# First attention's values written in token order and gathered by group on load, and the merge's row tiles taken in the order 1, 2, 0, 3

## What is computed

```python
DILATED_GROUPS = ((128, 1), (512, 4), (2048, 16))
...
qkv = proj[..., :QKV_COLS].astype(f32).reshape(
    B, S, 3, N_GROUPS, ATTN_HEADS_PER_GROUP, HEAD_DIM)
for g, (window, dilation) in enumerate(DILATED_GROUPS):
    num, den, mx = dilated_group_attention(
        qkv[:, :, 0, g], qkv[:, :, 1, g], qkv[:, :, 2, g], table_g, window, dilation)
...
m_all = jnp.max(jnp.stack(maxes), axis=0)
wts = [jnp.exp(mx - m_all) for mx in maxes]
num_tot = sum(w[..., None] * n for w, n in zip(wts, nums))
den_tot = sum(w * d for w, d in zip(wts, dens))
o_attn = num_tot / den_tot[..., None]
```

## Time and profile before

| what | value |
|---|---|
| median of 3 runs | 2580.51 us (2579.43 to 2581.24) |
| the profiled execution | 2580.89 us |
| its span, first to last instruction | 2578.7 us |
| mean granted TensorE clock | 0.996 |
| busy: TensorE matmuls, its weight loads | 2515.9 us (98%), 2050.9 us (80%) |
| busy: VectorE, ScalarE, GpSimd | 1353.0, 1048.6, 1126.6 us |

### The profile page before, as it was taken

The page is one execution under the profiler, slowest core; times in us unless marked ns, Lnnn a source line. Parts: engine busy times, 40 slices in busy tenths (PEclk is TensorE's granted clock), DMA queues, the critical chain, the costliest instruction groups (busy, mean ns, idle before and its releaser), DMA issues.

```text
span 2578.7 us, 41776 instructions
## 1 busy us (share of the span) xinstructions
PE 2515.9 (98%) x15936; PEld 2050.9 (80%) x15936; DVE 1353.0 (52%) x2579; ACT 1048.6 (41%) x2028; POOL 1126.6 (44%) x1390
## 2 busy tenths in 40 slices
PE   7999999999999999999999999899999999999999
PEld 6997777878777777777788778788887888777787
DVE  3002254345866657576532687676666007476733
ACT  4115656555433333242113453555554114455521
POOL 3332322223433233231457545576776455454452
PEclk9999999999999999999999999999999999999999
DMA  4241111211201111011432232233334114110132
GB/s 142 83 130 46 58 58 54 67 58 49 66 21 55 35 34 51 25 58 63 164 126 82 99 103 94 92 108 104 99 107 178 43 50 143 54 34 26 34 113 84
DMA packets 226566, 198.95 MB, mean 77 GB/s; under 512 B 7104, under 2 KB 193856, under 8 KB 225856
## 3 DMA queue, kind: packets, MB, share of 16 engines
q1 hardware_dynamic: 180928, 120.60, 15.2%
q10 hardware_dynamic: 45440, 75.68, 8.1%
HBM read 150.64 MB, written 45.61 MB: 76 GB/s over the span
## 4 chain that ended last, share of the span: by engine, by line
PE 84%; DVE 8%; ACT 4%; POOL 2%; issue 1%; DMA 0%; ACTq 0%; SPq 0%; DVEq 0%; POOLq 0%
PE gemm L799 14%; PE gemm L801 14%; PE gemm L800 13%; PE gemm L1260 5%; PE gemm L1262 5%; PE gemm L1261 5%; PE scores L871 2%; PE weighted L899 1%; PE scores L1464 1%; PE weighted L1488 1%; PE probs_t L884 1%; PE scores L1338 1%; PE probs_t L1131 1%; PE probs_t L1474 1%; PE scores L1035 1%
## 5 line engine op out<-in xcount | busy, mean ns | idle before, releaser
L749 POOL CAST w_hi<-w_raw 128x512 fp32r<-128x512 f32 x266 | 189.4, 712 | 1191.5 <-PE gemm L801 1034.9
L751 POOL TENSOR_TENSOR w_lo<-w_raw,w_hi 128x256 fp32r<-128x256 f32 x532 | 441.5, 830 | 42.1
L799 PE MATMUL gemm<-h_hi,w_hi 128*128 128x512 f32 x1072 | 449.0, 419 | 3.3 <-DVE h_lo L1956 3.3
L801 PE MATMUL gemm<-h_hi,w_lo 128*128 128x512 f32 x1072 | 420.1, 392 | 0.0
L800 PE MATMUL gemm<-h_lo,w_hi 128*128 128x512 f32 x1072 | 418.9, 391 | 0.0
L1609 DVE CUSTOM_DVE_ANT_0 neg_logits<-scores,bias_tile 128x128 f32<-128x128 f32 (+1 forms) x192 | 67.6, 352 | 344.7 <-PE scores L871 339.5
L799 PEld LDWEIGHTS gemm<-h_hi,w_hi 128*128 128x128 f32 x1072 | 202.1, 189 | 50.7 <-issue 14.2
L801 PEld LDWEIGHTS gemm<-h_hi,w_lo 128*128 128x128 f32 x1072 | 201.2, 188 | 44.1
L800 PEld LDWEIGHTS gemm<-h_lo,w_hi 128*128 128x128 f32 x1072 | 202.4, 189 | 32.5 <-issue 1.7
L799 PE MATMUL gemm<-xn_hi,w_hi 128*128 128x512 f32 x288 | 117.7, 409 | 1.9 <-DVE xn_lo L2236 1.7
L2476 ACT ACTIVATE prob<-neg_logits,row_max 128x128 f32<-128x128 f32 (+1 forms) x192 | 86.8, 452 | 76.7 <-DVE row_max L1609 72.0
(11 more groups left out here) (628 smaller groups left out, 6195.5 us busy)
## 6 DMA issues: line engine op xcount, KB each, us to landing
w_raw<-in_w_in SPq DMA_DIRECT2D x73, 512.0 KB, 3.9
w_raw<-in_a_w_in SPq DMA_DIRECT2D x28, 512.0 KB, 3.8
w_raw_b<-in_a_w_in SPq DMA_DIRECT2D x20, 512.0 KB, 4.7
gates_scratch<-o_f ACTq DMA_DIRECT2D x32, 256.0 KB, 2.0
merge_gates<-gates_scratch ACTq DMA_DIRECT2D x4, 2048.0 KB, 9.7
mlp_v_scratch<-v_piece ACTq DMA_DIRECT2D x32, 256.0 KB, 2.0
mlp_v<-mlp_v_scratch ACTq DMA_DIRECT2D x16, 512.0 KB, 3.9
w_raw<-in_a_w_out SPq DMA_DIRECT2D x16, 512.0 KB, 3.2
```

Source lines behind the costliest of these rows:

```text
L749: Q(pool.tensor_copy(weight_part(u, 0, ks), raw[:, s, ks, :]))
L751: Q(pool.tensor_tensor(weight_part(u, 1, ks), raw[:, s, ks, :], weight_part(u, 0, ks).bitcast(F32), ALU.subtract), E("w_split") if ks.stop ...
L799: pe.matmul(dst, w_high, hi(k, h), start=first, stop=False)
L801: m = pe.matmul(dst, w_low, hi(k, h), start=False, stop=last)
```

## The change

Block n of the values now holds the tokens 128n to 128n + 127 in every group, and `values_scratch` is laid out by token. The grouping is done by the load: SyncE issues two DMAs of 256 KB in place of one of 512 KB, with the rows of each group's order picked from DRAM, in pieces of 512 bytes for the groups 0 and 1 and 2 KB for group 2. Each raises the semaphore by 16, so that a pair and group now counts 48. The row tiles are taken in the order 1, 2 (first slot) and 0, 3 (second slot), in TensorE's and ScalarE's programs; the waits on `stat_in` and `stat_tr` are renumbered.

```diff
-        v1_d = nc.dram_tensor("values_scratch", (PAIRS, GROUPS, P, 8, P), F32).ap()
+        v1_d = nc.dram_tensor("values_scratch", (PAIRS, GROUPS, T, P), F32).ap()
...
-        stat_slots = {14 * p + 17 + j: [(p, 2 * j), (p, 2 * j + 1)] for p in range(PAIRS) for j in range(2)}
+        stat_slots = {14 * p + 17 + i: [(p, j) for j in ((1, 2), (0, 3))[i]] for p in range(PAIRS) for i in range(2)}
...
-        def tokens(ap, g, n):
-
-            if g == 0:
-                return ap[:, n * P:n * P + P]
-            r = STRIDE[g]
-            res, part = n // (8 // r), n % (8 // r)
-            return ap.rearrange("p (l r) -> p r l", r=r)[:, res, part * P:part * P + P]
...
-                    sp.dma_start(vrows[:, gi % 2, :, :], v1_d[gi // 3, gi % 3]).then_inc(bias_in[gi % 2], 16)
+                    values = v1_d[gi // 3, gi % 3]
+                    for part in range(2):
+                        if gi % 3 == 1:
+                            dst = vrows[:, gi % 2, part:8:2, :]
+                            src = values[HALF * part:HALF * part + HALF, :].rearrange("(j r) c -> j r c", r=4)
+                        elif gi % 3 == 2:
+                            dst = vrows[:, gi % 2, 4 * part:4 * part + 4, :]
+                            src = values.rearrange("(j r) c -> j r c", r=8)[:, 4 * part:4 * part + 4, :]
+                        else:
+                            dst = vrows[:, gi % 2, 4 * part:4 * part + 4, :]
+                            src = values[HALF * part:HALF * part + HALF, :].rearrange("(n j) c -> j n c", n=4)
+                        sp.dma_start(dst, src).then_inc(bias_in[gi % 2], 16)
...
-                        high, low = tokens(h1hi[:, 2 * kp + k, :], g, n), tokens(h1lo[:, 2 * kp + k, :], g, n)
+                        high, low = h1hi[:, 2 * kp + k, n * P:n * P + P], h1lo[:, 2 * kp + k, n * P:n * P + P]
...
                 if c % 12 == 0 and p > 0:
-                    pe.wait_ge(E("stat_in"), 4 * p)
+                    pe.wait_ge(E("stat_in"), 4 * p - 2)
...
-                if j == 3 or j == 0 and p > 0:
-                    pe.wait_ge(E("stat_in"), 4 * p if j == 0 else 4 * p + 1)
+                if j == 3:
+                    pe.wait_ge(E("stat_in"), 4 * p + 3)
...
-                act.wait_ge(E("stat_tr"), 4 * p + j + 1)
+                act.wait_ge(E("stat_tr"), 4 * p + (1, 2, 0, 3).index(j) + 1)
...
-                act.dma_start(v1_d[:, g, :, n, :].rearrange("x p c -> p x c"), v_stage[n][:]).then_inc(E(f"load_{n}"), 16)
+                act.dma_start(v1_d[:, g, n * P:n * P + P, :].rearrange("x p c -> p x c"), v_stage[n][:]).then_inc(E(f"load_{n}"), 16)
```

More of the change, by code:

```diff
@@ L405, in build @@
         V_OUT = (("x_again_v_out0", 16 * KT), ("oa_in_v_out1", 16 * PAIRS), ("oa_out_v_out2", 16 * (PAIRS - 1)), ("gate_out_v_out3", 32 * 16))
-        BIAS_LOADS, UP_LOADS, C_LOADS, T_HIGHS = 32 * PAIRS * GROUPS // 2, 32, 32, 20
+        BIAS_LOADS, UP_LOADS, C_LOADS, T_HIGHS = 48 * PAIRS * GROUPS // 2, 32, 32, 20
         LOADED = (80, 80, 80, 80, 64, 64, 64, 64)
@@ L880, in transposes @@
                 gi = 3 * p + g
-                pe.wait_ge(bias_in[gi % 2], 32 * (gi // 2 + 1))
+                pe.wait_ge(bias_in[gi % 2], 48 * (gi // 2 + 1))
                 for i, hh, ti in quad:
@@ L1599, in biased @@
                 dve.wait_ge(E("s_full"), c + 1)
-                dve.wait_ge(bias_in[gi % 2], 32 * (gi // 2 + 1))
+                dve.wait_ge(bias_in[gi % 2], 48 * (gi // 2 + 1))
                 if c > 0:
```

## The result

| | median (lowest to highest) | ratio to before, 95% interval |
|---|---|---|
| before, 4 runs | 2580.88 us (2579.43 to 2582.05) | |
| changed kernel, 4 runs | 2597.89 us (2595.42 to 2598.61) | 1.0065 [1.0052, 1.0078] |

The change costs 17.0 us. The profiled execution of the changed kernel took 2595.42 us, the lowest of its four: 14.53 us over the profiled execution of before. Its span is 2593.3 us and its mean granted clock 0.992; the clocks of the other three were 0.989 to 0.991.

The account below looks back on a forecast made before the run. TensorE was taken to bound the kernel, with ScalarE's copies ending last at the row tiles. Terms -5.1 + 0 + 18.0 - 4.0 + 6.2 = +15.1 us gave 2595.6 us against the median, range 2588 to 2600.

Parts of the forecast that it names:

- Part 1: Values' matmuls on TensorE: token order shortens weight loads, saving 5.1 us, 1.6 in group 1 and 3.5 in group 2.
- the rule of the free stride: Values, group 1: a stride up to 4 float32 costs nothing, so only 3.5 us saved, 2597.2 us; chance 0.02.
- Part 2: Gather on load: 12 more DMAs on SyncE cost 0, covered by 21.4 us between issue and first need.
- Part 3: Row tiles: TensorE's tile 3 waits for ScalarE's copy of tile 0 in shared bank `MB`, four stops, +18.0 us.
- Old stops: Ahead of the next pair's first scores: TensorE's three waits for the last tile copy vanish, -4.0 us.
- I take the whole 5.5: Last pair: its 5.5 us stop is charged in full, as blend, head sums and decay scan move with TensorE.
- rival 5: Last pair's stop partly swallowed by the VectorE and ScalarE chain behind it; half of 5.5 back, 2592.8 us; chance 0.08.
- Bounds: 0 if none falls, 6.2 if all do: Clock behind the four tile 3 stops: falls to 0.50, 1.56 us lost each, +6.2 us charged.
- Rival 1: Tile 3 stops come but the clock holds behind them: +8.9, 2589.4 us; chance 0.12, with a fall behind only some.

Follow-up runs that it names:

- values_only: Changed kernel with the old order of the row tiles and its waits, keeping token-order values and the gather on load: 2576.03 us, 0.9981 of before.
- before_relaxed: Kernel before, with TensorE's wait ahead of the next pair's first scores asking for three tiles copied in place of four: 2576.99 us, 0.9986 of before.
- busy_stop: Changed kernel with 15, 17, 18 and 22 unused matmuls between tile 0 and tile 3 in the four pairs: 2588.47 us, 1.0030 of before.
- own_bank: Changed kernel with tile 3 written to the bank of the transposed probabilities, so not waiting for tile 0's copy: 2571.49 us, 0.9963 of before.
- group1_strided: Changed kernel with group 1 reading every fourth token again, its values stored by group: 2598.97 us, 1.0070 of before.
- late_loads: Changed kernel with each pair's third value load issued one place later in SyncE's order: 2597.41 us, 1.0065 of before.
- tiles_only: Kernel before with only the row tiles' order changed to 1, 2, 0, 3, values as before: 2602.34 us, 1.0083 of before.
- relaxed_wait: New values, old tile order and banks; TensorE's wait ahead of the next pair's scores asks for three tiles copied, not four: 2572.20 us, 0.9968 of before.

## Why the prediction was right

The forecast was 2595.6 us, the measured median 2597.89, inside the forecast's own range; the direction and the mechanism are as told. By its steps:

- **Part 1, -5.1 us.** Measured -5.09 us in the trace, -4.7 in values_only. Group 1's share, against the rule of the free stride, is measured alone: 1.6 us.
- **Part 2, 0.** Right. The loads land in 3.9 to 4.8 us. Issuing one takes 0.46 us (median) in place of the 0.34 assumed, which nobody waits for.
- **Part 3, stops +18.0.** 3.85, 4.25, 4.43, 5.49 forecast; 3.80, 4.21, 4.41, 5.40 measured, 17.8 in all. The working held because ScalarE's copies could be read off the trace of before at the place where tile 2 had been.
- **Old stops -4.0.** Their line is gone. Part of the same gain is to be had without the change (before_relaxed).
- **"I take the whole 5.5".** Slightly too much: 1.0 us comes back in the blend. The prediction looked at the first spread of the weights only; the fifth one waited for VectorE before, and of that wait most is gone (timeline of TensorE, before and changed):

```profile
655.83 0.47 PE L922 MATMUL max_rows<-weight_rows_last,pick 128*128 128x512 f32 x1 [1.04 <-DVE numer L1654]
```

```profile
669.61 0.47 PE L925 MATMUL max_rows<-weight_rows_last,pick 128*128 128x512 f32 x1 [0.37 <-DVE numer L1657]
```

  So rival 5 was right in kind and came to 1.0 us in place of 2.7. busy_stop against own_bank has both effects in it, 17.8 - 1.0 = 16.8, measured 17.0.
- **"Bounds: 0 if none falls, 6.2 if all do".** This is the term that was mis-sized. All four fell. They cost 6.6 us in the profiled execution and 9.4 in the medians. The price of a fall was taken from one row of before, 1.56 us behind a stop of 2.94, and then used as a ceiling. But falls are not of one length. In the profiled execution of group1_strided, pair 0's stop is the same as in the changed kernel (3.66 us against 3.65), yet the clock is low for longer:

```profile
288.00:290.00 2.00, 1.37 (x6) 0.50 0.04 12
290.00:292.00 2.00, 2.00 (x6) 0.50 0.83 217
292.00:294.00 2.00, 2.00 (x6) 0.50 1.13 345
294.00:296.00 2.00, 2.00 (x8) 0.85 0.22 81
```

In the changed kernel's profiled execution it is nearly back by the second window:

```profile
290.00:292.00 2.00, 2.00 (x10) 0.98 1.05 323
```

From tile 3 to the next scores group1_strided needs 8.8 us (timeline of TensorE, below) and the changed kernel 7.5 (294.43 - 286.95). Such a longer fall costs 1.3 us more.

```profile
288.63 1.04 PE L916 MATMUL max_rows<-consts_sb,row_den 128*66 128x128 f32 x4 [3.66 <-ACT rows_max L2493]
...
297.45 0.93 PE L874 MATMUL scores<-k_t,q_t 64*128 64x128 f32 x8
```

The same stretch can be read in every kernel that has the four stops, and set against own_bank, where the clock holds (us from the start of tile 3 to the next pair's first scores; in pair 3 to the first product behind the attention):

| profiled execution | pair 0 | pair 1 | pair 2 | pair 3 | over own_bank, sum |
|---|---|---|---|---|---|
| own_bank | 6.00 | 6.00 | 6.00 | 22.32 | |
| changed | 7.48 | 7.62 | 8.08 | 23.94 | 6.80 |
| late_loads | 7.59 | 7.62 | 8.32 | 24.05 | 7.26 |
| tiles_only | 7.64 | 8.45 | 8.27 | 24.01 | 8.05 |
| group1_strided | 8.82 | 8.54 | 8.31 | 24.04 | 9.39 |

The stops ahead of tile 3 are the same in all four to 0.02 us, and the clock behind them costs 6.8 to 9.4 us. (The 6.6 above is the changed kernel's 6.8 set against the kernel before instead.) The changed kernel's profiled execution has the cheapest falls of the four; its other three runs show a lower mean clock (0.989 to 0.991 beside 0.992) and take 1.9 to 3.2 us more. That they had just such longer falls is argued from their clocks, since only one execution of each kernel has a trace.

A part of the closeness of the total, 2.3 us, is luck: this term was too low by 3.2 us (6.2 against 9.4), and the last pair's was too high by 1.0. What would have mended it: an upper bound well over a single fall's price, such as twice, since I had one row for it and no reason for a ceiling.

The fastest versions are own_bank (2571.49) and relaxed_wait (2572.20). Both beat the kernel before by 9 us and can't be told apart; relaxed_wait is the simpler one.

## What to carry to other kernels

When work is reordered, list for each step the buffer that it writes and who empties it: two steps on one bank, one behind the other, cost the whole copy, whatever the order gains elsewhere. Check also that a wait names only the copies of the buffer about to be written; here a constant one too high cost 3.4 us, and with the new values setting it right was worth as much as the new order with a bank of its own. And a stop of TensorE can cost more than its length, here by half as much again (9.4 us on 17.0 in four stops), so it pays to have other work stand in it: 12 matmuls of the next product put there (tile3_mid_half) took 2.7 us off each stop and three of the four falls with it.

## What the hardware did that I had not expected

- The clock's fall behind a stop of the same length differs between profiled executions of two kernels: behind 3.65 and 3.66 us in pair 0 it cost 1.4 us in the changed kernel and 2.7 in group1_strided. What decides it is not shown.
- Nor does a stop's length alone tell whether the clock falls right behind it. Further on, both kernels stop for 2.29 us ahead of the same product. Here are the changed kernel's row and window (timeline of TensorE; window):

```profile
1255.96 0.70 PE L802 MATMUL gemm<-o_hi,w_hi 128*128 128x512 f32 x1 [2.29 <-DVE merge_gates L1892]
```

```profile
1256.00:1258.00 2.00, 1.52 (x3) 0.51 1.03 438
```

  And the same product in the kernel before, where the clock was still full and fell some 3 us later, behind one more stop of 1.42 us (the changed kernel has such a second stop too, of 0.81):

```profile
1241.66 0.47 PE L799 MATMUL gemm<-o_hi,w_hi 128*128 128x512 f32 x1 [2.29 <-DVE merge_gates L1889]
```

```profile
1242.00:1244.00 2.00, 0.60 (x3) 1.00 1.00 422
1244.00:1246.00 2.00, 1.89 (x5) 0.65 1.04 442
```

  Rival 1 of the prediction leaned on the two falls behind stops over 2.5 us. The kernel before has one behind a shorter stop too, of 2.33 us, while the stop of 2.26 in the earlier trace rows left the clock full:

```profile
1991.64 0.47 PE L799 MATMUL probs_t<-mlp_y_hi,w_hi 128*128 128x512 f32 x1 [2.33 <-POOL w_lo L751]
```

```profile
1992.00:1994.00 2.00, 2.00 (x7) 0.53 0.67 203
```

- The low clock can begin inside the stop, and as long as TensorE stands idle it costs no time. In pair 3 of the changed kernel TensorE stands idle until 634.86 us, and this window has no matmul and a granted clock of 0.50:

```profile
632.00:634.00 2.00, 0.00 (x0) 0.50 0.61 250
```

- A gathered load of 256 KB in pieces of 512 bytes or 2 KB landed in 4.4 us (median), less than a contiguous one of 512 KB (4.9), while SyncE needed 0.46 us to issue it in place of 0.34.
